# Attention's product with V turned round: V stationary, two heads as column tiles of the array, the result already transposed for the output projection

## The reference, cut to what matters

```python
N_HEADS = 8; QK_HEAD_DIM = 96; V_HEAD_DIM = 64; Q_BLOCK = 128
def one_block(qblk):                                # 128 queries, all 8 heads
    s = jnp.einsum('bqhd,bhkd->bhqk', qblk, kt).astype(jnp.float32) * scale
    p = jax.nn.softmax(s, axis=-1).astype(vt.dtype)
    return jnp.einsum('bhqk,bhkd->bqhd', p, vt)
...
out_lat = jnp.concatenate([o_lat, fourier_mix(f_l, w_fourier)], axis=-1) @ w_out
x = x + g1 * mix_lat
f_lat = modulate(rms_norm(x, norm_ffn[l]), sh2, sc2)
```

## Time and profile before

| | us |
|---|---|
| median of 3 runs | 2723.68 |
| lowest and highest | 2714.36, 2724.6 |
| span of the profiled execution, first to last instruction | 2709.9 |
| median above that span | 13.8 |
| TensorE busy in the span | 2348.9 (87%) |
| VectorE, ScalarE, GpSimd busy | 1105.0, 620.8, 383.3 |
| the V product's matmuls (L771), busy | 309.1 |
| transposes of the probabilities (L751), busy | 217.1 |
| output projection (L802), busy | 257.6 |

### The profile page before, as it was taken

The page is one execution under the profiler, slowest core; times in us unless marked ns, Lnnn a source line. Parts: engine busy times, 40 slices in busy tenths (PEclk is TensorE's granted clock), DMA queues, the critical chain, the costliest instruction groups (busy, mean ns, idle before and its releaser), DMA issues. The chain is left out here.

```text
span 2709.9 us, 30557 instructions
## 1 busy us (share of the span) xinstructions
PE 2348.9 (87%) x9676; PEld 1365.1 (50%) x9677; DVE 1105.0 (41%) x2043; ACT 620.8 (23%) x1256; POOL 383.3 (14%) x372
## 2 busy tenths in 40 slices
PE   6899869999999948999887799599999997599990
PEld 1255446777775534444421455367777654344440
DVE  0045555444541143333334355644454312433335
ACT  0133334333331110111100243333333211011110
POOL 0033300000003311001011243100000032010002
PEclk9899989999999978999999899799999998699995
DMA  9401005000012216657789111020000121578845
GB/s 346 160 25 52 26 16 206 9 8 9 9 41 100 93 69 225 234 186 279 286 332 391 46 41 33 20 74 9 8 9 7 70 92 71 200 252 277 294 169 186
DMA packets 164581, 336.04 MB, mean 124 GB/s; under 512 B 10726, under 2 KB 91644, under 8 KB 163756
## 3 DMA queue, kind: packets, MB, share of 16 engines
q1 hardware_dynamic: 121388, 215.67, 22.5%
q10 hardware_dynamic: 30464, 73.50, 7.0%
q0 software_dynamic: 12672, 46.14, 4.8%
HBM read 271.65 MB, written 72.02 MB: 127 GB/s over the span
## 5 line engine op out<-in xcount | busy, mean ns | idle before, releaser
L880 PE MATMUL PS<-KV,R 128*128 x832 | 381.5, 613 | 30.3 <-DMA KV<-in_w_down 9.2
L745 PE MATMUL PS<-KV,R 96*128 96x512 f32 (+1 forms) x800 | 327.6, 518 | 4.8 <-ACT ZO L1061 3.6
L771 PEld LDWEIGHTS PS<-KV,R 128*128 128x128 f32 x2624 | 315.5, 192 | 11.0 <-issue 3.3
L771 PE MATMUL PS<-KV,R 128*128 128x64 f32 x2624 | 309.1, 272 | 2.6 <-ACT R L1058 1.3
L880 PEld LDWEIGHTS PS<-KV,R 128*128 128x128 f32 x832 | 160.6, 196 | 245.1 <-issue 245.1
L802 PE MATMUL PS<-KV,R 128*128 128x512 f32 x576 | 257.6, 601 | 2.7 <-ACT R L1078 2.7
L1461 DVE COPY R<-PS 128x256 f32<-128x256 f32 (+1 forms) x272 | 149.6, 550 | 248.8 <-PE PS L751 248.8
L1449 DVE TENSOR_REDUCE sm<-PS 128x1 f32<-128x1280 f32 (+1 forms) x144 | 197.7, 1373 | 123.1 <-PE PS L745 123.1
L751 PE MATMUL PS<-CST,R 128*128 128x128 f32 x1312 | 217.1, 279 | 15.7 <-ACT R L1050 1.9
L751 PEld LDWEIGHTS PS<-CST,R 128*128 128x128 f32 x1312 | 154.8, 147 | 113.3 <-ACT ZO L1061 43.0
L625 PE MATMUL PS<-KV,SC 128*2 128x512 f32 x384 | 174.5, 613 | 29.3 <-DMA KV<-in_w_ada 25.2
(11 more groups left out here) (232 smaller groups left out, 2445.8 us busy)
## 6 DMA issues: line engine op xcount, KB each, us to landing
KV<-in_w_ada ACTq DMA_DIRECT2D x22, 2048.0 KB, 19.2
KV<-in_w_gate SPq DMA_DIRECT2D x32, 1024.0 KB, 9.2
KV<-in_w_up SPq DMA_DIRECT2D x32, 1024.0 KB, 11.3
KV<-in_w_down SPq DMA_DIRECT2D x32, 1024.0 KB, 13.4
yb_d<-R ACTq DMA_DIRECT2D x52, 512.0 KB, 6.8
xmid_d<-R SPq DMA_DIRECT2D x18, 512.0 KB, 2.6
f_d<-R SPq DMA_DIRECT2D x18, 512.0 KB, 2.8
R<-xnext_d SPq DMA_DIRECT2D x18, 512.0 KB, 4.0
```

The source lines that it names most:

```text
L745: mm = pe.matmul(bank(b + i, 0, w), QS[0:QK, h, :], kT[0:QK, h, 512 * i:512 * i + w], start=True, stop=True)
L771: mm = pe.matmul(bank(7, 0, VDIM), pT[h % 2][:, j, :], V[:, j * 512 + h * VDIM:j * 512 + (h + 1) * VDIM], start=(j == 0), stop=(j == nk - 1))
L880: mm = pe.matmul(bank(2 + u), bT[u][:, kk, :], KV[:, bass.ds(off + kk * 512, 512)], start=(kk == 0), stop=(kk == KD - 1))
```

## The change

The probabilities are divided by their sum before they are transposed: VectorE, in a new function `norm`, takes the reciprocal and multiplies the head's 128x1280 probabilities in place. TensorE waits for that (`pn_ready`) before it transposes. VectorE keeps only the copy of chunk 2, ScalarE copies chunks 0 and 1.

The V product is done after every odd head, for two heads at once. V is stationary now (128 keys by 64 columns) and `pT` moves (128 columns); the even head writes partitions 0 to 63 and the odd head partitions 64 to 127 of the free columns 256 to 383 of bank 2, one after the other for each of the ten key blocks. The result has two heads' features in partitions and 128 tokens in columns. ScalarE copies it once a pair to `OT`, which lies where `ZO` lay, and the projection reads its stationary pieces straight from `OT` and from the Fourier half `FT`. `stage`, `otrans`, `oev`, `mx` and `Ost` are gone. TensorE's part of the projection is written out for all tiles in place of a loop. Because bank 2 is shared with the even heads' scores, the V product waits until the exponential of the next head has read its scores (`p_ready`), and an even head's last scores wait until the pair's result has been copied (`o_ready`).

The core of the diff (`one` is the next head, `two` the head after next):

```diff
-        xd0, xd1, tg, ff0, ff1, fTb, mx0, mx1, Ost = take([D, D, D, D, D, D, D, D, 512])
-        xd, mx = [xd0, xd1], [a.rearrange("p (k n) -> p k n", k=KD) for a in (mx0, mx1)]
+        OT = ZO.rearrange("p (k n) -> p k n", k=HEADS // 2)
+        xd0, xd1, tg, ff0, ff1, fTb = take([D, D, D, D, D, D])
+        xd = [xd0, xd1]
...
                     mm.then_inc(pT_ps[ci], 1)
 
-                def attend(n, h, nk, tile, nxt):
+                def attend(n, h, nk, tile, one, two):
                     s = HEADS * n + h
-                    pe.wait_ge(p_ready, s + 1)
+                    pe.wait_ge(pn_ready, s + 1)
+                    ge(pe, pT_ready[0], s)
+                    if nk > 4:
+                        ge(pe, pT_ready[2], s - CS)
                     transposes(h, nk, 0)
-                    ge(pe, o_ready, s)
                     if nk > 4:
+                        ge(pe, pT_ready[1], s - CS)
                         transposes(h, nk, 1)
-                    if nxt:
-                        scores(*nxt, parts=(0,))
+                    if two:
+                        scores(*two, parts=(0,))
                     if nk > 4:
                         pe.wait_ge(pT_ready[0], s + 1)
                         transposes(h, nk, 2)
-                    if nxt:
-                        scores(*nxt, parts=(1, 2))
+                    if two:
+                        if h % 2 == 0:
+                            ge(pe, o_ready, HEADS // 2 * n + h // 2)
+                        scores(*two, parts=(1, 2))
+                    if h % 2 == 0:
+                        return
+                    if one:
+                        pe.wait_ge(p_ready, s + 2)
                     for ci in range(-(-nk // 4)):
                         pe.wait_ge(pT_ready[ci], s + 1 - (CS if ci else 0))
                     for j in range(nk):
-                        mm = pe.matmul(bank(7, 0, VDIM), pT[h % 2][:, j, :], V[:, j * 512 + h * VDIM:j * 512 + (h + 1) * VDIM],
-                                       start=(j == 0), stop=(j == nk - 1))
+                        for z in range(2):
+                            mm = pe.matmul(PS[z * VDIM:(z + 1) * VDIM, 2, 256:256 + P],
+                                           V[:, j * 512 + (h - 1 + z) * VDIM:j * 512 + (h + z) * VDIM], pT[z][:, j, :],
+                                           start=(j == 0), stop=(j == nk - 1))
                     mm.then_inc(o_ps, 1)
 
-                n0 = context_steps(l, attend, scores)
+                def ahead(n0, h0, k0, n1, h1, k1):
+                    scores(n0, h0, k0)
+                    scores(n1, h1, k1)
+
+                n0 = context_steps(l, attend, ahead)
                 with pe.Fori(0, LAT_TILES - 1) as j:
                     lat_steps(attend, j + n0, j + CTX_TILES, False)
...
-
-                def otrans(t, u, DB=DB, t0=t0):
-                    d = t + (DB - t0)
-                    pe.wait_ge(o_staged, d + 1)
-                    ge(pe, oT_ready, d)
-                    for kk in range(4):
-                        mm = pe.transpose(bank(4, kk * P, (kk + 1) * P), Ost[:, kk * P:(kk + 1) * P], ident)
-                    mm.then_inc(oT_ps, 1)
 
                 def project(t, u, half, DB=DB, t0=t0):
                     d = t + (DB - t0)
                     if half == 0:
-                        pe.wait_ge(oT_ready, d + 1)
-                        pe.wait_ge(fx_ready, d + 1)
                         ge(pe, gx_ready, d - 1)
                     for kk in range(KD):
-                        mm = pe.matmul(bank(2 * u + half), mx[u][:, kk, :], wout[:, kk, half * 512:(half + 1) * 512],
+                        mix = OT[:, kk, t * P:(t + 1) * P] if kk < 4 else FT[:, kk - 4, t * P:(t + 1) * P]
+                        mm = pe.matmul(bank(2 * u + half), mix, wout[:, kk, half * 512:(half + 1) * 512],
                                        start=(kk == 0), stop=(kk == KD - 1))
                     if half == 1:
...
 
 
-                def dstep(t, h, u, routed=True, normed=True, last=False):
-                    project(t, u, 0)
-                    if routed:
+                def dstep(t):
+                    project(t, t % 2, 0)
+                    if t >= t0 + 2:
                         route(t - 2)
-                    project(t, u, 1)
-                    if not last:
-                        otrans(t + 1, 1 - u)
-                    if normed:
-                        ftrans(t - 1, 1 - u)
-                otrans(t0, 0)
-                dstep(t0, t0 // 2, 0, routed=False, normed=False)
-                dstep(t0 + 1, t0 // 2, 1, routed=False)
-                loop(pe, None, t0 + 2, TILES - 2, dstep)
-                dstep(TILES - 2, 0, 0)
-                dstep(TILES - 1, 0, 1, last=True)
+                    project(t, t % 2, 1)
+                    if t > t0:
+                        ftrans(t - 1, 1 - t % 2)
+                for t in range(t0, TILES):
+                    dstep(t)
                 route(TILES - 2)
                 ftrans(TILES - 1, 1)
...
                                    ).then_inc(p_ready, 1)
 
-                def attend(n, h, nk, tile, nxt):
+                def attend(n, h, nk, tile, one, two):
                     s = HEADS * n + h
+                    w = min(4, nk)
+                    act.wait_ge(pT_ps[0], s + 1)
+                    act.activation(pT[h % 2][:, 0:w, :].rearrange("p j n -> p (j n)"), bank(6, 0, w * P), ACT.Copy).then_inc(pT_ready[0], 1)
                     if nk > 4:
                         act.wait_ge(pT_ps[1], s + 1 - CS)
                         act.activation(pT[h % 2][:, 4:8, :].rearrange("p j n -> p (j n)"), bank(7), ACT.Copy).then_inc(pT_ready[1], 1)
-                    act.wait_ge(rinv, s + 1)
-                    act.wait_ge(o_ps, s + 1)
-                    act.activation(ZO[:, bass.ds(tile * 512 + h * VDIM, VDIM)], bank(7, 0, VDIM), ACT.Copy,
-                                   scale=sm[:, 54 + h % 2:55 + h % 2]).then_inc(o_ready, 1)
-                    if nxt:
-                        soft(*nxt)
-
-                n0 = context_steps(l, attend, soft)
+                    if two:
+                        soft(*two)
+                    if h % 2 == 1:
+                        act.wait_ge(o_ps, HEADS // 2 * n + h // 2 + 1)
+                        act.activation(OT[:, h // 2, bass.ds(tile * P, P)], bank(2, 256, 256 + P), ACT.Copy).then_inc(o_ready, 1)
+
+                def ahead(n0, h0, k0, n1, h1, k1):
+                    soft(n0, h0, k0)
+                    soft(n1, h1, k1)
+
+                n0 = context_steps(l, attend, ahead)
                 with act.Fori(0, LAT_TILES - 1) as j:
...
                     act.activation(fT[:, 0:4, :].rearrange("p k n -> p (k n)"), bank(5), ACT.Copy).then_inc(fTa, 1)
 
-                def dact(t, h, u, first=False, last=False):
-                    if not last:
-                        oev(t + 1, 1 - u)
+                def dact(t, h, u, first=False):
                     if not first:
                         fTev(t - 1, 1 - u)
                     frms(t, u)
                 dact.steps = 1
-                oev(t0, 0)
                 dact(t0, 0, 0, first=True)
                 dact(t0 + 1, 0, 1)
...
                 mixer_steps(pool, None, step)
 
                 DB = 0 if l == 0 else TILES
-                pool.wait_ge(o_ready, HEADS * (TILES * l + 1))
-
-                def stage(t, u, DB=DB, t0=t0):
-                    d = t + (DB - t0)
-                    ge(pool, oT_ps, d)
-                    carry()
-                    pool.tensor_copy(Ost, ZO[:, bass.ds(t * 512, 512)]).then_inc(o_staged, 1)
-                    ge(pool, op_ps, d - 1)
-                    carry()
-                    pool.tensor_copy(mx[u][:, 4:8, :], FT[:, :, bass.ds(t * P, P)]).then_inc(fx_ready, 1)
-
                 def resid(t, h, u, DB=DB, t0=t0):
                     d = t + (DB - t0)
...
                     dve.tensor_scalar(sm[:, 50 + h % 2:51 + h % 2], sm[:, 48 + h % 2:49 + h % 2], -SCALE, None, ALU.mult).then_inc(nmax, 1)
 
-                def attend(n, h, nk, tile, nxt):
+                def norm(n, h, nk):
                     s = HEADS * n + h
                     dve.wait_ge(p_ready, s + 1)
-                    ge(dve, o_ready, s - 1)
-                    dve.reciprocal(sm[:, 54 + h % 2:55 + h % 2], sm[:, 52 + h % 2:53 + h % 2]).then_inc(rinv, 1)
-                    for ci in (0, 2):
-                        j0, j1 = 4 * ci, min(4 * ci + 4, nk)
-                        if j1 > j0:
-                            dve.wait_ge(pT_ps[ci], s + 1 - (CS if ci else 0))
-                            dve.tensor_copy(pT[h % 2][:, j0:j1, :].rearrange("p j n -> p (j n)"),
-                                            bank(6, 0, (j1 - j0) * P)).then_inc(pT_ready[ci], 1)
-                    if nxt:
-                        vmax(*nxt)
-
-                n0 = context_steps(l, attend, vmax)
```

(46 more changed lines are left out.)

25 lines of the change are left out of this document (4 added, 21 removed).

## The result

The changed kernel takes 2737.14 us (median of 4 runs, 2733.79 to 2741.35) against 2719.02 for the kernel before: ratio 1.0073, 95% interval 1.0048 to 1.0097. It is slower, by about 0.7%, where faster was forecast. The profiled execution has a span of 2739.4 us and took 2741.35.

What follows compares the result with a forecast made beforehand. TensorE was taken to bound attention and projection. Savings of 30 (62 pairs at 0.49), 4 (layer ends) and 12.5 (projection) sum to 47 us: span 2709.9 to 2663, plus 13.8 gives 2677 us; range 2660 to 2755.

Steps and rivals of the forecast that it cites:

- what the V product pays for: Attention's V product pays for loading 128 columns; turned round, with full tile overlap, a pair takes 2.2 us, not 4.36.
- Rivals 1 and 2: V product: 1, tiles take turns, 4.36 us, time 2804, chance 0.17; 2, half overlap, 3.3 us, time 2736, chance 0.08.
- the copy of chunk 0: Odd steps: ScalarE's copy behind the exponential holds chunk 2 until 3.88 us after the scores, TensorE idle 2.14.
- The even side: Pair's stretch from V product to next chunk 2: TensorE's work 3.94 us, ScalarE's chain 4.13 and so 0.2 longer.
- Rival 5: Attention: no wait for chunk 0, pair tends to 8.7 us, time about 2535; chance 0.03 for this or better.
- the pair at the full clock: Two heads of latent attention repeat in 11.05 us, 0.49 less than 11.54; 62 pairs give 30 us.
- rival 3: Array empties at each change of tiling, pausing 0.20 us before and after each V product: time 2689, chance 0.12.
- rival 4: Clock falls in attention's new idle time; behind one pair in three 36 us, time 2713; chance 0.20.
- Context heads: The 16 heads with two key blocks only: longer chain against fewer results and products, 0, bounds 3 us either side.
- the end of the last layer's attention: One V product less seen, 2.2 us a layer; the way to the first projection saves 1.9.
- The projection: TensorE-bound; four transposes fewer a tile (0.44), 1.9 and 1.28 saved at each layer's first two tiles: 12.5 us.
- The 13.8 us around the span: Runs' median taken to lie 13.8 us above the profiled span, added to span 2663 to give 2677 us.

Runs made afterwards that it cites:

- kernel 2: Changed kernel with the V product's two loops exchanged, ten products of the even head, then ten of the odd: 2889.36 us (one run).
- Kernels 3, 4 and 7: 3: changed kernel, ScalarE copies before exponential in odd steps, 2650.51 us; 4: kernel 3 plus VectorE's copy before scaling, 2603.08; 7: kernel 4 plus even-step scores earlier, 2573.12.
- kernel 8: Changed kernel with the turned V product made after each head, one tile, bank 7, chunk 0 copied by VectorE, result taken before the exponential: 2724.61 us.
- Kernel 1: Changed kernel with four dummy 256-column products in TensorE's idle time before chunk 2 of odd steps: 2683.7 us, ratio to the kernel before 0.9882.
- kernel 6: Changed kernel with eight dummy 128-column products right ahead of the V product, the 1.97 us idle stretch left as it was: 2895.95 us (one run).
- kernel 5: Changed kernel with one dummy 256-column product (0.43 us) before chunk 2 of odd steps: 2685.97 us, ratio to the kernel before 0.9904.

## Why the prediction was wrong, point by point

**Right: what the V product pays for.** Full overlap was taken at 2.2 us for 40 instructions; it is 2.34, and 4.13 with the tiles in turn (kernel 2), for which 4.36 stood in the text. Rivals 1 and 2 are refuted.

**Right: the copy of chunk 0.** Forecast 3.88 us from the even step's scores to chunk 2, measured 3.87; idle forecast 2.14, shown as 1.97. The even side was forecast at 4.13 and measures 4.13 (1927.43 to 1931.56), but that is luck: the forecast had TensorE done after 3.94 and waiting 0.2 for ScalarE's copy, while in the trace the copy ends at 1931.33, TensorE shows no idle time, and its own pieces fill the 4.13 (2.34 for the V product, 1.79 for transposes and first scores). Kernels 3, 4 and 7 take the wait away piece by piece and the pair goes 11.17, 10.57, 9.76, 9.29. Rival 5 is refuted.

**Nearly right: the pair at the full clock,** 11.05 forecast, 11.17 measured. The 0.12 more lies ahead of the V product: from chunk 2 to its start are 1.66 us (1925.77 to 1927.43) where 1.52 was counted, 0.09 of it because it starts 1.39 us behind the start of the last scores, here as in kernel 8, where 1.30 was counted. At its other end it takes 0.15 more than its 20 slots, which went into the slack of the even side. Together that is about 0.24 us for a V product, where rival 3 had set 0.40. No run isolates what it is. The Trainium skill (TensorEngine Tiling (Array Packing), Tiling Modes, Key Properties) says that a change of tiling mode drains TensorE; edges of 0.09 and 0.15 us agree with that and don't prove it.

**Wrong: the clock.** This is the step that turned a gain into a loss. The forecast's sum has the clock at 1.00 through attention and no term for it, on the strength of "a gap of 3.25 us was followed by 1.00"; rival 4, the fall of the clock in the new idle time, had a chance of 0.20 and a price of 36 us, behind one pair in three. The clock falls behind one pair in two: mean 12.02 against 11.17, 0.85 a pair. Kernel 1 takes that away alone, with 53 us, and kernel 6 shows that it is the idle place. A row that warned of it was in the list, the fall to 0.50 after gaps of 0.6 and 0.7 us at the end of attention. I set it beside the long single gap in a stretch of dense products, where it should have counted for more, since in the new pair too the idle time stands between transposes and a few scores. That it is this neighbourhood that makes the rows alike is my reading; no run tests it. With rival 4 at its measured 53 us, the forecast's 2677 would have been 2730.

**Terms besides.** *Context heads* were taken at 0, with bounds of 3 us. The first layer's attention has lost 6.2 us more than the last's (20.7 against 14.5), which is put down to them. A pair of context heads takes 3.41 us at the full clock and 4.27 at half, where two heads took 3.11 before. TensorE's waits in a pair at the full clock, for VectorE's scaling and for ScalarE's copy of chunk 0:

```profile
432.45 0.41 PE L752 MATMUL PS<-CST,R 128*128 128x128 f32 x2 [0.51 <-DVE R L1433]
...
433.89 0.66 PE L782 MATMUL PS<-R,KV 128*64 128x128 f32 x8 [0.59 <-ACT R L1059]
```

A stretch of 13.7 us at half clock lies over the first of these pairs. In kernel 5, whose instructions are the same there, they all take 3.41, and the first latent pair's V product starts 43.90 us behind the layer's first scores, against 47.98 in the changed kernel and 45.96 in kernel 1. So about 4 of the 6 us are the clock, and not in every execution.

*The start of a layer's attention* had no term. In the last layer the first pair's V product starts 18.08 us behind the first scores, where the second head's started after 14.71; TensorE waits 2.85 us for the first scaling, where it waited 1.07 for the first exponential, and then has 3.4 us at half clock:

```profile
1795.55 1.96 PE L752 MATMUL PS<-CST,R 128*128 128x128 f32 x8 [2.85 <-DVE R L1433]
```

That is 3.4 us lost. At the end of the last layer's attention 3.9 us were to be won (2 of the V product, 1.9 of the way to the first projection), and 3.9 were: from the third V product from the end to the first projection it was 14.02 us, and from the last but one, which answers to it, it is 10.13.

*The projection.* Of the forecast's 12.5 us, 3.8 lie ahead of the first projections, so 8.7 are to be laid beside the 12.8 of the stage's rows. Of these, 2.3 are the clock's and were not forecast: before, the first tile of the last layer's stage took 17.45 us, with the half clock of the earlier trace rows in it, and that of the first layer's 15.13; in the changed kernel the clock doesn't fall there. The rest is 0.58 a tile instead of 0.44, as half a projection takes 6.87 us where it took 7.03 and 6.95. The scaling takes 0.887 us (0.91 forecast) and is covered in the latent pairs.

**The balance.** The span went up by 29.5 us and was to go down by 47, 76 apart: the clock 53, the pair at full clock 62 x 0.12 = 7, the context heads 6, the start of the two layers' attention 7 (3.4 each, if the first layer's is like the last's) and 7 in stages that the change doesn't touch, together 80, less 4 that the projection's rows won more than forecast. The 53 and the 6 share about 2 us, as kernel 1 also ran some of the context heads at a higher clock.

**The 13.8 us around the span** don't exist, and that term of the sum was wrong: in each of the later executions the span lies 1.8 to 2.2 us below the time. The profiled execution of the kernel before was a short one: its 2709.9 us of span make an estimated 2712 in time, below all four of its timed runs. So the forecast's terms, laid on the median of 2719 us, give about 2672 in place of 2677, and of the 29.5 us between the two spans only 18 stand between the medians. The other 11 us are differences between single executions, and the rows for stages that the change doesn't touch (7 us) and for the clock in the context heads (4 us) are where they are to be looked for. Kernel 1's 2684, near the forecast, is in part luck too: without the clock's 53 us the terms above still differ, and partly cancel.

## What to carry to other kernels

When work that used to lie over a chain of other engines is made cheaper or gathered into every second step, write down what covers the chain in each step of the new order, and move the copy that frees a bank ahead of the long instruction on its engine: the same change, with two such moves and a third of the scores moved ahead of the wait, is 5.2% faster than before instead of 0.7% slower. Of an idle gap that comes again in each turn of a loop, look in the trace not for the longest gap that kept the clock, but for the shortest gaps behind which it was lost. A filler product in the gap is a cheap test that tells the gap's own cost from the clock's.

## What the runs showed of the hardware

- Two fp32 products in two column tiles of 64 run beside each other: 40 instructions with 128 moving columns in 2.34 us when they alternate, 4.13 when one tile's twenty come first.
- In this loop TensorE kept its full clock, but for three single stretches, with 1.54 us idle in each pair of 11.17 us (kernel 5), and lost it for 3.4 us in every 24 with 1.97 idle (the changed kernel). More work elsewhere in the pair, with the 1.97 idle as they were, did not bring it back (kernel 6, 0.88).
- 1.7 us of useless products a pair made the kernel 53 us faster (kernel 1), 0.43 us of them 51 us (kernel 5).
